# First norm from row sums, a reordered start of the loads, and sample rows on 32-column tiles in a one-layer decoder step

## What is computed

```
sh1,sc1,g1,sh2,sc2,g2 = split6(silu(c) @ w_ada + b_ada)
h  = RMSNorm(x)*(1+sc1)+sh1
[q|k|v|p|ga|gb] = h @ w_in
x  = x + g1 * ((sigmoid(ga)*(attention(q,k,v) @ w_branch_attn) + sigmoid(gb)*(pool(p) @ w_branch_pool)) @ w_out)
h2 = RMSNorm(x)*(1+sc2)+sh2
x  = x + g2 * PEER(h2)
```

## Time and profile before

| what | us |
|---|---|
| runs of the kernel before | 1817.88, 1819.41, 6214.62; median 1819.41 |
| the profiled execution, its own time | 1814.91 |
| its span, first to last instruction | 1813.0 |
| busy in the span: PE, DVE, ACT, POOL | 1250.6, 1109.7, 255.4, 1087.9 |
| mean granted clock of TensorE | 0.863 |

### The profile page before, as it was taken

How to read it: one execution, slowest core, us unless ns; L and a number is a source line. 1 busy time by engine, 2 the same in 40 slices (tenths; PEclk the granted TensorE clock), 3 DMA queues, 4 the chain that set the end, 5 groups by cost and what they waited for, 6 DMA issues and landing times.

```text
span 1813.0 us, 19530 instructions
## 1 busy us (share of the span) xinstructions
PE 1250.6 (69%) x7073; PEld 642.1 (35%) x7073; DVE 1109.7 (61%) x2615; ACT 255.4 (14%) x491; POOL 1087.9 (60%) x1066
## 2 busy tenths in 40 slices
PE   5999998985878577556877755465446556555487
PEld 3558676772544233112444411121112112111122
DVE  5015341677666677678666766776777777766613
ACT  2015511220111000110111200000010000100011
POOL 1111000157767777767777777777777777777764
PEclk8999989998989899778999967877886788778899
DMA  9434545799999999999999999999999999999996
GB/s 332 129 108 157 164 148 187 280 329 367 404 406 405 396 401 407 391 385 398 405 406 407 407 398 400 406 407 400 405 407 402 405 401 408 410 409 409 408 356 256
DMA packets 196409, 639.21 MB, mean 353 GB/s; under 512 B 21872, under 2 KB 23204, under 8 KB 196186
## 3 DMA queue, kind: packets, MB, share of 16 engines
q0 software_dynamic: 154992, 550.65, 77.7%
q1 hardware_dynamic: 41322, 87.31, 13.6%
HBM read 634.09 MB, written 3.59 MB: 352 GB/s over the span
## 4 chain that ended last, share of the span: by engine, by line
POOL 44%; PE 21%; DMA 16%; issue 15%; DVE 2%; ACT 1%; SPq 0%; DVEq 0%; POOLq 0%; PEldq 0%; ACTq 0%
POOL arena L564 44%; DMA arena<-in_peer_v,arena 12%; PE psum L1285 7%; PE psum L1625 4%; PE psum L1354 4%; DMA arena<-in_peer_u,arena 2%; DMA arena<-in_w_ada 1%; PE psum L1303 1%; PE psum L1637 1%; DMA arena<-in_w_in 1%; ACT arena L619 1%; DVE arena L1180 1%; DMA arena<-in_x_sample 0%; PE psum L1671 0%; PE psum L1311 0%
## 5 line engine op out<-in xcount | busy, mean ns | idle before, releaser
L1625 PE MATMUL psum<-arena 64*64 64x512 f32 x4096 | 640.3, 769 | 504.5 <-DMA arena<-in_peer_v,arena 482.2
L1180 DVE CUSTOM_DVE_ANT_0 arena<-arena 128x1024 f32<-128x1024 f32 x520 | 636.2, 1228 | 405.0 <-DMA arena<-in_peer_u,arena 389.0
L564 POOL DMA_INDIRECT arena<-in_peer_u,arena x520 | 541.1, 1041 | 222.7 <-issue 155.2
L564 POOL DMA_INDIRECT arena<-in_peer_v,arena x520 | 521.1, 1002 | 203.1 <-issue 145.8
L1625 PEld LDWEIGHTS psum<-arena 64*64 64x64 f32 x4096 | 200.0, 172 | 918.9 <-issue 808.8
L1285 PE MATMUL psum<-arena 128*128 128x264 f32 (+2 forms) x1592 | 365.4, 386 | 8.1 <-DMA arena<-in_w_branch_pool 6.3
L1285 PEld LDWEIGHTS psum<-arena 128*128 128x128 f32 x1592 | 296.2, 192 | 89.7 <-issue 37.0
L619 ACT ACTIVATE arena<-psum 128x512 f32<-128x512 f32 (+7 forms) x218 | 88.6, 446 | 481.3 <-PE psum L1285 313.1
L778 ACT ACTIVATE arena<-arena 128x16 f32<-128x16 f32 x32 | 6.9, 217 | 817.2 <-DVE arena L1180 817.2
L1354 PE MATMUL psum<-arena 128*128 128x512 f32 (+1 forms) x192 | 72.1, 536 | 4.3 <-DMA arena<-in_w_in 4.3
L1354 PEld LDWEIGHTS psum<-arena 128*128 128x128 f32 x192 | 37.0, 194 | 39.2 <-issue 32.6
(11 more groups left out here) (207 smaller groups left out, 762.5 us busy)
## 6 DMA issues: line engine op xcount, KB each, us to landing
arena<-in_w_ada SPq DMA_DIRECT2D x12, 2048.0 KB, 13.2
arena<-in_w_in SPq DMA_DIRECT2D x10, 2048.0 KB, 15.3
arena<-in_peer_wq SPq DMA_DIRECT2D x8, 2048.0 KB, 16.4
arena<-in_peer_u,arena POOLq DMA_INDIRECT x520
arena<-in_peer_v,arena POOLq DMA_INDIRECT x520, 7.6
arena<-in_w_out SPq DMA_DIRECT2D x4, 2048.0 KB, 16.9
arena<-in_w_branch_attn SPq DMA_DIRECT2D x4, 1024.0 KB, 11.4
arena<-in_w_branch_pool SPq DMA_DIRECT2D x2, 2048.0 KB, 13.9
```

The lines of the kernel that those rows point to most:

```text
L564: pool.indirect_dma_start(out=rows_to, out_offset=None, in_=table[0], in_offset=bass.IndirectOffsetOnAxis(ap=index, axis=0)).then_inc(land ...
L1180: dve.tensor_tensor_reduce(rows_r, rows_r, h, 1.0, 0.0, ALU.mult, ALU.add, total).then_inc(u_used, 1)
L1625: ins = pe.matmul(psum[i * HW:(i + 1) * HW, sums_bank(b) + 2 * g + h, :], diags[n % 4][ps, q % 2 * GS + k + i, :], v_rows[v_buf[r]][ps, h ...
```

## The change

The first norm's sums are taken by DVE from the loaded rows, one instruction per block, as each block lands. Root and reciprocal are taken on 5 columns of 128; the reciprocals go onto diagonals, which PE spreads over the partitions with the matrix of ones (`rstd`). The sample rows and the blocks of x are SP's first loads after `c`, with a semaphore each; identity and vectors move to POOL's queue, ahead of its small loads. POOL's wait before constants, `w_pool` and caches is now for the first block's q product. `ada_products(0)` and `(1)` follow each other. At the end, sample t goes to the 32-column tile t%4 with a matrix of 2 columns, two samples side by side; `fold(3)` is cut into `fold_rows` (before the first samples) and `fold_sums` (after the fourth). The samples' x and gates are brought to the same rows by 64 products in place of 16 transposes, and the samples' result is stored in 4 transfers of 2 rows.

```diff
-    plan = [(("vecT",), "A"), (("cT",), "A")]
-    plan += [(("xT", c), "A") for c in range(C)] + [(("xTs",), "A")]
-    plan += ada_rows(0) + [(("ss", 1, h), "V") for h in both]
-    plan += ada_rows(1) + ada(0) + ada_rows(2) + ada(1) + ada_rows(3) + ada(2) + ada(3)
+    plan = [(("cT",), "A"), (("xTs",), "A")]
+    plan += [(("xT", c), "A") for c in range(C)] + [(("rstd", h), "V") for h in both] + [(("vecT",), "A")]
+    plan += ada_rows(0) + ada_rows(1) + ada(0) + ada_rows(2) + ada(1) + ada_rows(3) + ada(2) + ada(3)
...
-        sp.dma_start(kc[:, 0:K_IOTA], consts[:, 0:K_IOTA]).then_inc(ident_loaded, 16)
-        sp.dma_start(vec68[0:48, :], b_ada[0].rearrange("(a b) -> a b", b=P)).then_inc(vecs_loaded, 16)
-        sp.dma_start(vec68[48:56, :], norm1_g[0].rearrange("(a b) -> a b", b=P)).then_inc(vecs_loaded, 16)
-        sp.dma_start(vec68[56:64, :], norm2_g[0].rearrange("(a b) -> a b", b=P)).then_inc(vecs_loaded, 16)
-        sp.dma_start(vec68[64:68, :], pool_scale[0].rearrange("(a b) -> a b", b=P)).then_inc(vecs_loaded, 16)
+        sp.dma_start(xnat[0:S, NB, :], x_sample[:, 0, :]).then_inc(x_loaded[NB], 16)
         for b in range(NB):
-            sp.dma_start(xnat[:, b, :], x_prompt[0, b * P:(b + 1) * P, :]).then_inc(x_loaded, 16)
-        sp.dma_start(xnat[0:S, NB, :], x_sample[:, 0, :]).then_inc(x_loaded, 16)
+            sp.dma_start(xnat[:, b, :], x_prompt[0, b * P:(b + 1) * P, :]).then_inc(x_loaded[b], 16)
...
-        sp.dma_start(y_sample[:, 0, :], g2s_rows[0:S, :]).then_inc(sample_y_stored, 16)
+        for j in range(4):
+            sp.dma_start(y_sample[j:S:4, 0, :], g2s_rows[32 * j:32 * j + 2, :]).then_inc(sample_y_stored, 16)
...
+        pool.dma_start(kc[:, 0:K_IOTA], consts[:, 0:K_IOTA]).then_inc(ident_loaded, 16)
...
-        wait_filled(pool, ("ada_rows", 2))
+        wait_filled(pool, ("q", 0))
...
             copy(("xT", c), xT[:, c, 0:T], bank(("xT", c)))
-        copy(("xTs",), xT[:, :, T:TT], bank(("xTs",))[:, 0:64].rearrange("p (a b) -> p a b", a=C))
+            if c == 0:
+                act.wait_ge(x_mean_ready, 1)
+                act.activation(x_mean, x_mean, ACT.Sqrt).then_inc(root_ready, 1)
...
-        for c in range(C):
-            wait_emptied(dve, ("xT", c))
-            link(dve.tensor_tensor(squares_all[:, c, 0:T], xT[:, c, 0:T], xT[:, c, 0:T], ALU.mult))
-            if c:
-                add_squares(squares_all, c, slice(0, T))
-        wait_emptied(dve, ("xTs",))
-        link(dve.tensor_tensor(squares_all[:, :, T:TT], xT[:, :, T:TT], xT[:, :, T:TT], ALU.mult))
-        link(dve.tensor_reduce(res_s, squares_all[:, :, T:TT].rearrange("p c s -> p s c"), X, ALU.add))
-        dve.tensor_copy(squares_all[:, 0, T:TT], res_s).then_inc(square_sum_ready, 1)
-        mean_squares(1, 0)
-        mean_squares(1, 1)
-        normalize(1, slice(0, TT))
+        link(dve.memset(x_mean, 1.0))
+        for b in (NB, 0, 1, 2, 3):
+            dve.wait_ge(x_loaded[b], 16)
+            r = rows(b)
+            ins = dve.tensor_tensor_reduce(x_squares[b][0:r], xnat[0:r, b, :], xnat[0:r, b, :], 1.0, 0.0, ALU.mult, ALU.add, x_mean[0:r, b:b + 1])
+        link(ins)
+        dve.tensor_scalar(x_mean, x_mean, 1.0 / D, EPS, ALU.mult, ALU.add).then_inc(x_mean_ready, 1)
+        dve.wait_ge(root_ready, 1)
+        dve.wait_ge(ident_loaded, 16)
+        link(dve.reciprocal(x_mean, x_mean))
+        for b in range(NB):
+            dve.tensor_scalar(x_diag[:, cols(b)], ident, x_mean[:, b:b + 1], None, ALU.mult)
+        dve.tensor_scalar(x_diag[0:S, T:TT], ident[0:S, 0:S], x_mean[0:S, NB:NB + 1], None, ALU.mult).then_inc(x_diag_ready, 1)
+        for h in range(2):
+            wait_filled(dve, ("rstd", h))
+            ins = dve.tensor_copy(root[:, half(h)], bank_half(("rstd", h), h))
+            ins.then_inc(emptied_by_dve, 1)
+        wait_emptied(dve, ("rstd", 1))
+        wait_emptied(dve, ("xT", C - 1))
+        scale_columns(slice(0, TT))
+        wait_emptied(dve, ("vecT",))
         for i in range(4):
...
-            dve.tensor_tensor(coef_s[:, 0:S * S:S + 1], act_s, gate_s, ALU.mult).then_inc(sample_coef_ready, 1)
+            dve.tensor_tensor(coef_s[:, 0:S:2], act_s[:, 0:4], gate_s[:, 0:4], ALU.mult)
+            dve.tensor_tensor(coef_s[:, S + 1:2 * S:2], act_s[:, 4:8], gate_s[:, 4:8], ALU.mult).then_inc(sample_coef_ready, 1)
...
+        pe.wait_ge(x_diag_ready, 1)
+        for h in range(2):
+            o = begin(("rstd", h))
+            for i in range(2):
+                b = 2 * h + i
+                ins = pe.matmul(o[:, i * P:(i + 1) * P], ones, x_diag[:, cols(b)], start=True, stop=True)
+            if h:
+                ins = pe.matmul(o[:, 2 * P:2 * P + S], ones[0:S, :], x_diag[0:S, T:TT], start=True, stop=True)
+            end(ins)
+        pe.wait_ge(vecs_loaded, 16 * 4)
+        end(pe.transpose(begin(("vecT",))[:, 0:68], vec68[0:68, :], ident[0:68, 0:68]))
         wait_emptied(pe, ("cT",))
         ada_products(0)
-        pe.wait_ge(ones_ready, 1)
-        pe.wait_ge(square_sum_ready, 1)
-        for h in range(2):
-            mean_squares(1, h, squares_all[:, 0, half(h)])
...
-            for t in (2 * q, 2 * q + 1):
+            pair = (2 * q, 2 * q + 1)
+            for t in pair:
                 r = sample_row(t)
                 pe.wait_ge(v_landed[v_buf[r]], v_landing[r])
-                for h in range(2):
-                    ins = pe.matmul(psum[0:S, 6 + h, :], coef_s[:, t * S:(t + 1) * S], v_rows[v_buf[r]][:, h * 512:(h + 1) * 512],
-                                    start=(t == 0), stop=(t == S - 1), skip_group_check=True)
-                ins.then_inc(v_used, 1)
-            if q == 3:
-                pe.wait_ge(v_used, sample_row(S))
-                pe.nop().then_inc(sample_out_ready, 2)
-
-        def fold(b):
+            for h in range(2):
+                for t in pair:
+                    j = t % 4
+                    ins = pe.matmul(psum[32 * j:32 * j + 2, 6 + h, :], coef_s[:, 2 * t:2 * t + 2], v_rows[v_buf[sample_row(t)]][:, h * 512:(h + 1) * 512],
+                                    start=(t < 4), stop=(t >= 4), skip_group_check=True)
+            ins.then_inc(v_used, 2)
+
+        def fold_rows(b):
...
                               start=(c == 0), stop=False, skip_group_check=True)
+            return o
+
+        def fold_sums(b, o):
             for h in range(2):
...
-                        ins = pe.transpose(psum[0:S, 6 + c // 4, c % 4 * P:(c % 4 + 1) * P], src[:, c, first:first + S], ident)
+                        for j in range(4):
+                            ins = pe.matmul(psum[32 * j:32 * j + 2, 6 + c // 4, c % 4 * P:(c % 4 + 1) * P], src[:, c, first + j:first + S:4], ident,
+                                            start=True, stop=True, skip_group_check=True)
...
             if p - 2 == SAMPLES_AT:
+                if q == 0:
+                    last = fold_rows(NB - 1)
                 combine_samples(q)
                 if q == 1:
-                    fold(NB - 1)
+                    fold_sums(NB - 1, last)
```

More of the change, by code:

```diff
@@ L396, in decoder_layer @@
     idx_s, gate_s, act_s = at(take(S), S).bitcast(I32), at(take(S), S), at(take(S), S)
-    coef_s = at(take(S * S), S * S)
+    coef_s = at(take(2 * S), 2 * S)
     assert top[0] <= o_mT1 + C * late[1]
@@ L637, in ada @@
             copy(("ada_rows", i), ada_rows[i], bank(("ada_rows", i)))
-        ada(0)
-        wait_emptied(act, ("ss", 1, 1))
-        act.activation(root, msq, ACT.Sqrt).then_inc(root_ready, 1)
-        for i in range(1, 4):
+        for i in range(4):
             ada(i)
@@ L900, in ada, with scale_columns @@
                               bias, ALU.add).then_inc(emptied_by_dve, 1)
+        def scale_columns(cs):
+            for c in range(C):
+                ins = dve.tensor_tensor(hT[:, c, cs], xT[:, c, cs], root[:, cs], ALU.mult)
+            link(ins)
         def normalize(n, cs):
@@ L1314, in _ @@
         pe.wait_ge(ident_loaded, 16)
-        pe.wait_ge(vecs_loaded, 16 * 4)
-        end(pe.transpose(begin(("vecT",))[:, 0:68], vec68[0:68, :], ident[0:68, 0:68]))
         pe.wait_ge(silu_ready, 1)
@@ L1321, in _ @@
         end(ins)
-        pe.wait_ge(x_loaded, 16 * 5)
-        for c in range(C):
-            o = begin(("xT", c))
-            for b in range(NB):
-                ins = pe.transpose(o[:, b * P:(b + 1) * P], xnat[:, b, c * P:(c + 1) * P], ident)
-            end(ins)
+        pe.wait_ge(x_loaded[NB], 16)
         o = begin(("xTs",))
@@ L1701, in _ @@
             if k in (AT_ROWS, 4 * (2 * PH + 3), 4 * (3 * PH + 3)):
-                fold(p // PH - 1)
+                fold_sums(p // PH - 1, fold_rows(p // PH - 1))
     block.__exit__(None, None, None)
```

43 lines of the change are left out of this document (28 added, 15 removed).

## The result

| what | before | after |
|---|---|---|
| median of 11 runs, us | 1819.41 | 1810.94 |
| ratio after to before | | 0.9939, 95% interval 0.9921 to 0.9957 |
| profiled execution, own time | 1814.91 | 1811.03 |
| its span | 1813.0 | 1808.9 |
| first `peer_u` fetch, last `peer_v` fetch issued at | 347.17, 1790.08 | 343.61, 1794.19 |

What follows compares the result with a forecast made beforehand. POOL's 1040 serial fetches hold the chain and keep their length; the change acts at both ends. Start 5.5 plus end 5.4 gives 10.9 us off the 1819.41 median: 1808.5 us, range 1799 to 1820 for 8 in 10.

Steps and rivals of the forecast that it cites:

- only the start: Rival at the end: two 2-column tiles don't overlap, three stores cost 1.2 us, only the start gains; 1815.1 us, chance 0.09.
- only the end: Rival at the start: a load not moving with PE uses up its gain before the fetches; 1814.0 us, chance 0.11.
- The clock stays up: Rival at the start: PE's idle stretches become too short for half clock, start gains 8.5 us; 1805.5 us, chance 0.12.
- 5.2 was the term: Start: 2.0 MB of constants and w_pool now wait for the first q product, freeing 5.2 us of DMA.
- Piece 3 of `w_ada` ends 10.8 MB into the loads: Start: the piece's load, summed by bytes, was to end at 33.3 us, where before it was put at 34.6.
- q products at about 39.5: Start, sign of being right: PE's first product with the q piece of w_in at about 39.5 us, before at 44.92.
- Four such quarters are 7.5 us: End: samples' products run two side by side, each quarter 1.87 us; 7.5 us instead of 14.1, 6.6 less.
- 1.2 us for three stores: End: the result's store becomes four issues; three more at 0.30 to 0.47 us each cost 1.2 us.
- DMA does not take over: End: the last rows have landed by 1796 us, the last quarter starts about 1799.5, so DMA does not become the bound.
- I take 8 us: Samples' x and gates: 64 products, 128 records, take 8 us, 6 more than before, all hidden; range 7.7 to 33.
- The room: Behind the samples' turn: combine may be 9.8 us late before POOL's fetch into the peer_v buffers must wait.
- the slower rival: Samples' turn: 128 records run singly at half clock, combine 31 us late, POOL waits about 21; 1829.5 us, chance 0.08.

Runs made afterwards that it cites:

- tail_only: The kernel before with only the samples' part of the change (coefficient matrix to the four stores); 1817.27 us, ratio 0.9957 to the kernel before.
- start_only: The changed kernel with the samples' part at the end taken back to that of before; 1818.64 us, ratio 0.9981 to the kernel before.
- small_late: The changed kernel with POOL's last small loads (q and k norm gains, sinks; 68 KB) held until the first q product; 1805.79 us, ratio 0.9907.
- small_late_again: The same kernel as small_late, run once more beside the unedited changed kernel on one chip; 1809.60 us, ratio 0.9924.
- changed_again: The changed kernel as it is, run and profiled once more; 1810.22 us, ratio 0.9925 to the kernel before.
- one_tile: The changed kernel with all eight samples on one 32-column tile instead of four, so their rows add into one another; 1817.20 us, ratio 0.9969.
- turn_x8: The changed kernel with each of the 64 products that turn the samples' x and gates issued eight times; 1831.45 us, ratio 1.0052.
- caches_early: The changed kernel with POOL's old wait before constants, w_pool and caches, so they load at their old place; 1814.33 us, ratio 0.9946.
- fold_early: small_late with the turn of the last x block (fold_rows) moved ahead of the last combine; 1806.53 us, ratio 0.9917.

## Why the prediction was right, step by step

**What bounds it, and that both ends count**: right. `tail_only` shows the end alone, so the rival "only the start" falls. The start alone is not shown by `start_only`, whose interval takes in 1, and its first fetches overlap with the old ones (341.3 to 350.4 in five profiles, 347.2 and 349.8 in two). What is shown is that its q products come earlier, and that a start made earlier still reaches the time: `small_late` (0.9889 to 0.9925) and `small_late_again` (0.9896 to 0.9952) lie below the 0.9957 of the end alone, the first of them clear of its interval. So "only the end" falls too, though the 3.5 us of the start are known only roughly. "The clock stays up" falls: from 36 to 45 us it stood at 0.53 in after, and from 23 to 38 us at 0.77 to 0.89 in the four other profiles of this start.

**The start, 5.5 forecast, 3.9 measured.** The q products of the five profiles with the changed start and POOL's small loads early (after, `changed_again`, `start_only`, `one_tile`, `turn_x8`: 44.04, 42.01, 41.38, 41.70, 41.61) have a mean of 42.1; the two of the old start (44.92, 47.19) 46.1. That is 3.9 us, and at the first fetch it is 344.7 against 348.5, 3.8. The mechanism was right. The constants' bytes took the time: with them back in their place (`caches_early`) the q products came 4.9 us later than that mean, and 5.2 was the term. The dip at 32 to 36 is gone.

The step that failed is "Piece 3 of `w_ada` ends 10.8 MB into the loads", which gave 33.3 us for the fourth `w_ada` product. It began at 35.49 to 36.11 in the five profiles. The bytes up to 32 us were as forecast: 8 x 228 + 4 x 170 + 20 x 388 GB/s are 10.3 MB, against 10.0 before, so of the 0.7 us counted for the earlier issue of x 0.6 were there. But by 35.69 it is 11.7 MB, 0.9 more than piece 3 and all ahead of it. They can only be of the next pieces, those of `w_in`, which SP issued at 25.56 and 33.69. The sum had the pieces one behind the other, and PE free to start with the last byte of its own; here 0.9 MB of the next ones, 2.3 us at 388 GB/s, had moved before it started. Whether the pieces move side by side, or PE hears of the last byte that much later, the runs don't tell. In `tail_only`, with the old start, the fourth product waited for its piece until 36.16, where the sum had 34.6.

From there to the q products 5.6 or 7.3 us were forecast (38.9 or 40.6 less 33.3), by the clock; 5.9 us were measured in the four profiles that ran it at full clock, and 8.4 in after, with the clock at half for nearly all of it. So "q products at about 39.5" was wrong by 2 to 5 us, and the fetches weren't "5 to 6 us earlier throughout".

A second thing had no term at all: POOL's small loads were counted by their bytes, 0.3 MB with the vectors. With 68 KB of them held back, the fourth product began at 32.79 to 33.10 in six profiles, 2.8 us earlier. The kernel before paid for them too: there POOL's queue, which held only these, took 7.2% of the DMA engines' time in the first 40 us, 2.9 us. The change moved them from ahead of x to among its blocks, where from 8 to 12 us they took 2.3 us of it.

**The end, 5.4 forecast, 8.3 measured.** Two terms were mis-sized. (The 0.88 us of a product is one of 16 in 14.08, not of 8; the sum isn't touched by it.) "Four such quarters are 7.5 us": a quarter by itself does take 1.89, but the two quarters of a half lie on four different tiles and run side by side too where their rows are there, 1.92 for both; the sum was 5.1. And the tail behind PE, sized as before plus 1.2 us for three stores: from the end of the last product to the end of the span it is 5.5 us, against 1813.0 - 1808.1 = 4.9 before, so 0.6. That DMA does not take over was right in the changed kernel, where the fold fills the time, but only just: `fold_early` waits for the rows, and at 1796 to 1798 us DMA now moves 412 GB/s, where 6 stood before.

The Trainium skill ("TensorEngine Tiling (Array Packing)", Tiling Modes, Key Properties) says that a change of the tiling mode drains the array; the forecast put at most 0.2 us on each. In the trace of after the products on 32 columns begin at 1801.49, when the 3.70 us of the 128-column ones from 1797.86 are just over, and take the same 1.92 us as in the earlier trace rows: no drain is to be seen there, as far as modelled ends can show one. The order of the products has three such changes, not the four that the forecast counted.

**The middle.** "I take 8 us" for the 128 records: they took 4.4, below the 7.7 that I had as the cheapest, since 64 records took 1.93 us, 30 ns each, half of the row it was sized by the earlier trace rows. Six microseconds or two, all of it is hidden. The room is confirmed to about a microsecond, and so is the price of the slower rival: its 1829.5 is 1.0055 of the median before, and `turn_x8`, where its 31 us were really there, had 1.0052.

**The median.** The two errors, 1.6 us too much at the start and 2.9 too little at the end, nearly cancel: 12.2 us by the stages, 10.9 forecast. That 11.1 was measured by the ratio is luck twice over: the errors cancel, and the measurement itself is no better than some 3 us (8.5 by the medians; the second one, `changed_again`, had 13.7 by its ratio and 12.5 by the medians).

**What stays open.** Why the 1040 fetches of one program last 1450.6 us in one execution and 1445.8 in another (after and `changed_again`), 1445.1 and 1448.9 (`small_late`, `small_late_again`). It is not the start, since the old one had 1442.9 and 1448.2, and it is as large as the start's gain; a single profile can't show a gain of this size, as the 3.9 us of the first pair showed.

## What to carry to other kernels

Work out a change in the stage that it touches, and the room behind what grows from the buffer that is waited for: the room held here to about a microsecond, where the time of the whole scatters by ten and more. Where several loads are on their way, look how many bytes of the ones behind have moved when the one that is waited for is there: a sum of the bytes ahead of it came out 2.3 us early here. Small loads that are moved to another queue still run on the same DMA engines: put them behind the large ones that the path waits for. Products on different 32-column tiles are worth bringing together in the order: here they overlapped only when they followed one another.

## What the runs showed of the hardware

**Small loads hold up large ones.** The DMA queues in the first 40 us of after, by packets, MB and share of the 16 engines:

```profile
q1 hardware_dynamic: 6277, 13.13, 88.7%
q0 software_dynamic: 320, 0.18, 8.5%
```

POOL's queue (the small loads, with identity and vectors) has 1.4% of the bytes and 8.5% of the time. From 8 to 12 us alone it took 57.4% of the engines' time for 0.07 MB, in `small_late` 0.4%; from 10 to 12 us PE and DVE ran nothing. The Trainium skill ("DMA: Bandwidth & Descriptors", Specifications) gives 512 bytes as the least transfer for full rate; the trace counts 396 packets below that in these 40 us, 116 of them from 8 to 12 us, where the rate was 170 GB/s, and agrees in direction.

**Four tiles give nearly all of four.** 16 records of 512 columns took 7.03 us on one tile and 1.92 on four, 3.7 times as fast; two records by themselves took 1.05. The other surprise is the size of the clock's share: 16 records take 2.05 or 3.78 us, and the same program falls on either side from one execution to the next.
